# Score blocks of 32 by 32 on four column groups, attention's second product four heads at a time, and a reordered convolution

## The chip, the cores and the metric

One core of one Trainium2 chip runs the whole program. The metric is the device time of one execution in microseconds (us); for several runs it is their median. TensorE (PE) is the matrix engine, VectorE is DVE in the profile, ScalarE is ACT, GpSimd is POOL, SyncE (SP) issues most transfers.

## What is computed

Two transformer blocks follow each other on 256 tokens of width 1024, everything in float32. Two pieces matter here. In the first block each of 16 attention heads (8 "fox", 8 "swa") of width 64 computes

```python
p = jax.nn.softmax(logits, axis=-1)                  # 256 queries, causal or windowed
return jnp.einsum('bhqk,bkhd->bqhd', p.astype(v.dtype), v)
```

beside a short convolution `gate_b * conv(gate_c * u)` over 512 channels and six gates. In the second block a gated linear recurrence runs in both directions over 8 heads of 128:

```python
decay = jnp.exp(jnp.minimum(diff, 0.0)) * mask[:, :, None]
scores = jnp.einsum('bhtk,bhsk,bhtsk->bhts', qc, kc, decay)
o_intra = jnp.einsum('bhts,bhsv->bhtv', scores, vc)
```

All large weights (about 180 MB) are read once from memory. Each large product is made of three cheap products (high part by high part, high by low, low by high).

## The kernel before

**Units.** A weight of 128 by 2048 elements is a unit. SP loads it into `raw`, ACT copies it to its rounded part `whi` (`hi`, L1214), DVE forms the rest `wlo` (`lo`, L1844), PE multiplies (`unit`, L548, and `unit_tm`, L630). There are three buffers of each kind, and ACT and DVE work two units ahead of PE. Every engine has its own program, written out by hand; the engines wait for each other by counted semaphores. What stands between two units is called a slot below.

**Attention** (first block). In slot t PE does `values(t-4)`, `probs(t-3)` (three transposes, L823) and `scores(t-1)` (L811, L812). `values(i)` (L837, L838) multiplies one head's 128 tokens by 128 columns of values, of which 64 are the head's and 64 are zeros, so that two heads add up into one bank `Ob`. ACT makes exponentials and copies the turned probabilities (`pt`, two buffers, L1357); for every second head ACT and DVE split `Ob` into `y_hi` and `y_lo` (L1365, L1866). The units beside them are, in order, the convolution's `cc`, `cu`, `cb`, then six gates of two units each. DVE does the convolution as one piece after slot 5: `z` (L2035), three taps for each of four channel groups (L2039, L2043), then `lo` of the next unit.

**Recurrence scores** (second block). In each of two halves i (4 heads each), nine levels n = 0 to 8 with distances h = 0, 1, 2, 4, ..., 64, 128 are computed, one in each slot. `mix_exps` prepares on ACT and DVE the scaled keys `kt` and queries `qt` of level n and advances the running sums `xf`, `xb`, `pf`, `pb`. PE's `mix_scores` (L1026) computes for levels 0 to 7 sixteen blocks of 64 keys by 64 queries: 8 pairs, each pair's outputs on partitions 0 to 63 and 64 to 127 of a bank. DVE copies the entries that belong to the level into `an` by a mask (L2311), and at level 64 `an` into the diagonal blocks of `am` (L2306); ACT copies level 0, level 64 (L1572) and level 128 (L1578). `mix_values` (L1042) multiplies the scores `am` by `v`, 256 columns at a time.

**What sets the order.** In each recurrence slot ACT and DVE run `mix_exps(i, t)`, then `hi` or `lo` of the unit two ahead, then the copy of level t-1; PE runs the unit and then level t-1.

Of the kernel before, what the change touches and what calls it, by code (L numbers as in the profile page):

```python
# [4 lines left out]
F32 = mybir.dt.float32  # L5
F32R = mybir.dt.float32r
U8 = mybir.dt.uint8
# [25 lines left out]
def constants():  # L33
# [6 lines left out]
    for h in LEVELS[:-1]:  # L40
        same = (i[:, None] // (2 * h)) == (i[None, :64] // (2 * h))
        other = (i[:, None] // h) != (i[None, :64] // h)
        masks.append(np.tile((same & other)[:64], (2, 1)).astype(np.float32))
# [46 lines left out]
def build(nc, d, out):  # L90
# [20 lines left out]
    masks = at("masks", [P, 6, 64], U8, 91)  # L111
# [14 lines left out]
    mk = at("mk", [P, 6, 64], F32, 160)  # L126
# [4 lines left out]
    skf = at("skf", [P, 2, P], F32, 180)  # L131
    fv = [at(f"fv{u}", [P, 2, 4, P], F32, 184 + 4 * u) for u in range(2)]
# [13 lines left out]
    PT = [at(f"pt{i}", [P, 384], F32, 140.5 + 1.5 * i) for i in range(2)]  # L146
# [26 lines left out]
    Am = at("am", [P, 4, 2, T], F32, 156)  # L173
    An = at("an", [P, 8, 64], F32, 204)
# [151 lines left out]
    U["cc"], U["cu"], U["cb"] = (cols(w_in, c, 512, 8) for c in (512, 1024, 0))  # L326
    for i in range(6):
        U[f"gate{i}"] = cols(w_in, 3848 + 512 * i, 512, 8)
    wb = d["w_branch"].rearrange("a b k n -> (a b) k n")
# [80 lines left out]
    def sync(e):  # L410
# [51 lines left out]
        e.dma_start(mk[:, :, :], d["c_masks"].rearrange("p (l n) -> p l n", l=6)).then_inc(s_mk, 16)  # L462
        fetch_for("cu", "cb")
        for i in range(6):
            fetch_for(f"gate{i}")
        e.wait_ge(*pe_val.on(("attn", 15)))
        e.wait_ge(*v_split.on(("y", 15)))
# [52 lines left out]
    def tensor(e):  # L520
# [269 lines left out]
        def scores(i):  # L790
# [14 lines left out]
            if i == 8:  # L805
                e.wait_ge(*p_pad.on(("local value", 1)))
                e.wait_ge(*v_evac.on("sq"))
                e.wait_ge(*v_evac.on("sk"))
# [17 lines left out]
        def values(i):  # L826
            kind, h = heads[i]
            if kind == "fox":
                val = [fv[h % 2][:, t_, h // 2, :] for t_ in range(2)]
            else:  # L830
                val = [sv[h // 4][:, t_, :] for t_ in range(2)]
            e.wait_ge(*a_soft.on(("pt", i)))
            if i == 8:
                e.wait_ge(*a_evac.on("sv"))
            if i % 2 == 0 and i >= 2:
                e.wait_ge(*v_split.on(("y", i - 1)))
            e.matmul(Ob[:, 0:T], val[0], PT[i % 2][:, 0:T], start=i % 2 == 0, stop=False, skip_group_check=True)  # L837
            e.matmul(Ob[:, P:T], val[1], PT[i % 2][:, T:T + P], start=False, stop=True,  # L838
                     skip_group_check=True).then_inc(*pe_val.up(("attn", i)))

        def attention(t):
            if t >= 4:
                values(t - 4)
# [16 lines left out]
        linear("cb", HA, 1, None, v_evac.on("cc"), lambda i: attention(6 + i))  # L860
        for g in range(6):
            free = v_evac.on(("cu", "cb")[g]) if g < 2 else a_stat.on(("gate", g - 2))
            for i in range(2):
                unit_tm(f"gate{g}", i, HA, g % 2, free if i == 0 else None)
                attention(8 + 2 * g + i)
# [6 lines left out]
        e.wait_ge(*v_split.on(("y", 7)))  # L872
        unit_tm("br01", 0, Y, 0, a_stat.on(("gate", 4)), K=4, off=4)
        e.wait_ge(*v_split.on(("y", 15)))
# [126 lines left out]
        def mix_scores(i, n):  # L1001
# [1643 lines left out]
```

## Time and profile before

| what | value |
|---|---|
| median of 3 runs | 1052.52 us (1050.35 to 1052.54) |
| the profiled execution | 1050.1 us, of which the span from first to last instruction is 1048.3 us |
| PE matmuls | 1038.3 us busy, 99% of the span, 7132 records |
| DVE, ACT | 747.0 us (71%), 601.8 us (57%) |
| DMA | 182.84 MB, mean 174 GB/s |
| granted TensorE clock | 1.000 over the span |

A float32 product is two records of PE in the profile (a turning one is one record). Matmuls are pipelined and the ends of their records are modelled, so the distance between starts tells what a product costs, not the length of its record; a short wait of PE hides in that modelled tail, and a longer one stands in brackets only with what is left of it.

### The profile page before, as it was taken

Reading aid. Unit: us, or ns where it says so; the run is one execution under the profiler, and the core shown is the slowest. Engines: PE = TensorE matmul, PEld = TensorE weight load, DVE = VectorE, ACT = ScalarE, POOL = GpSimd, SP = SyncE. Lnnn points to the kernel's source line nnn. Section 1 sums busy time; section 2 is a strip of 40 time slices with the busy share of each in tenths; the row PEclk is TensorE's granted clock in tenths of the full one; section 3 lists DMA queues with packets and bytes.
Section 4 is the critical chain, followed back from the end, with each engine's and each line's share of the span. In section 5 each row is a group of like instructions: output and inputs, shape, how many; then the busy total and the mean of one; then the engine's idle time right before and its main releaser. Section 6 shows DMA issues by size and latency. Waiting matters only on the chain.

```text
span 1048.3 us, 16748 instructions
## 1 busy us (share of the span) xinstructions
PE 1038.3 (99%) x7132; PEld 943.7 (90%) x7132; DVE 747.0 (71%) x889; ACT 601.8 (57%) x736; POOL 8.0 (1%) x15
## 2 busy tenths in 40 slices
PE   9999999999999999999999999999999999999998
PEld 8999788889998988888899989999999888888887
DVE  5677765675654678776668898589948888776456
ACT  5564466435434565555447986698664765545443
POOL 3000000000000000000000000000000000000000
PEclk9999999999999999999999999999999999999999
DMA  9964344754543466565565555354444657554641
GB/s 295 229 187 167 121 161 161 210 193 160 201 161 122 160 217 208 188 201 172 175 215 162 161 161 162 121 161 153 139 154 152 199 170 231 176 189 159 222 160 41
DMA packets 141451, 182.84 MB, mean 174 GB/s; under 512 B 14133, under 2 KB 92065, under 8 KB 141377
## 3 DMA queue, kind: packets, MB, share of 16 engines
q1 hardware_dynamic: 141160, 181.57, 54.8%
q8 instruction: 56, 0.92, 0.3%
q10 hardware_dynamic: 216, 0.21, 0.1%
q14 instruction: 19, 0.15, 0.0%
HBM read 180.51 MB, written 1.25 MB: 173 GB/s over the span
## 4 chain that ended last, share of the span: by engine, by line
PE 88%; DVE 5%; ACT 4%; issue 2%; DMA 1%; SPq 0%; DVEq 0%; ACTq 0%
PE ps L548 26%; PE ps L581 22%; PE ps L630 15%; PE ps L583 11%; PE ps L674 2%; PE ps L1156 2%; PE ps L1026 1%; ACT whi L1214 1%; PE ps L578 1%; DVE wlo L1844 1%; PE ps L676 1%; DMA x_tm<-in_x 1%; PE ps L906 1%; PE ps L1042 1%; PE ps L928 1%
## 5 line engine op out<-in xcount | busy, mean ns | idle before, releaser
L1844 DVE TENSOR_TENSOR wlo<-raw,whi 128x2048 fp32r<-128x2048 f32 (+3 forms) x170 | 378.1, 2228 | 141.0 <-ACT whi L1214 140.5
L1214 ACT ACTIVATE whi<-raw 128x2048 fp32r<-128x2048 f32 (+1 forms) x167 | 310.5, 1863 | 84.2 <-PE ps L548 28.8
L548 PE MATMUL ps<-ha,whi 128*128 128x256 f32 x1264 | 232.1, 286 | 1.5 <-DVE wlo L1844 1.5
L581 PE MATMUL ps<-ha,whi 128*128 128x512 f32 x640 | 222.7, 395 | 0.0
L548 PEld LDWEIGHTS ps<-ha,whi 128*128 128x128 f32 x1264 | 197.6, 192 | 3.8 <-issue 1.6
L548 PE MATMUL ps<-ha,wlo 128*128 128x256 f32 x632 | 178.8, 283 | 0.0
L583 PE MATMUL ps<-ha,wlo 128*128 128x256 f32 x640 | 177.4, 277 | 0.0
L581 PEld LDWEIGHTS ps<-ha,whi 128*128 128x128 f32 x640 | 120.0, 188 | 28.0
L548 PEld LDWEIGHTS ps<-ha,wlo 128*128 128x128 f32 x632 | 121.1, 192 | 0.0
L583 PEld LDWEIGHTS ps<-ha,wlo 128*128 128x128 f32 x640 | 120.2, 188 | 0.1
L581 PE MATMUL ps<-pr,whi 128*128 128x512 f32 x330 | 115.3, 394 | 0.0
L630 PE MATMUL ps<-whi,ha 128*128 128x512 f32 x320 | 101.2, 397 | 0.2
L583 PE MATMUL ps<-pr,wlo 128*128 128x256 f32 x330 | 91.5, 277 | 0.0
L581 PEld LDWEIGHTS ps<-pr,whi 128*128 128x128 f32 x330 | 61.9, 188 | 13.7
L630 PEld LDWEIGHTS ps<-whi,ha 128*128 128x128 f32 x320 | 59.4, 188 | 13.1 <-issue 1.0
L630 PE MATMUL ps<-wlo,ha 128*128 128x512 f32 x160 | 62.5, 391 | 0.0
L583 PEld LDWEIGHTS ps<-pr,wlo 128*128 128x128 f32 x330 | 62.0, 188 | 0.0
L1513 ACT ACTIVATE silu<-silu 128x512 f32<-128x512 f32 x22 | 13.9, 633 | 62.3 <-DVE silu L2183 62.3
L1508 ACT ACTIVATE silu<-ps 128x512 f32<-128x512 f32 x22 | 13.1, 597 | 41.2 <-PE ps L583 35.3
L630 PEld LDWEIGHTS ps<-wlo,ha 128*128 128x128 f32 x160 | 30.0, 188 | 6.5
L2185 DVE TENSOR_TENSOR silu<-silu,rw 128x512 f32<-128x512 f32 x22 | 15.2, 692 | 15.9 <-ACT silu L1513 15.9
L1349 ACT ACTIVATE lb<-lb,sc 128x128 f32<-128x128 f32 x16 | 6.3, 394 | 30.6 <-DVE sc L1983 30.6
(406 smaller groups left out, 1744.2 us busy)
## 6 DMA issues: line engine op xcount, KB each, us to landing
raw<-in_w_in SPq DMA_DIRECT2D x54, 1024.0 KB, 5.2
raw<-in_w_ffn_gate SPq DMA_DIRECT2D x11, 1024.0 KB, 5.1
raw<-in_w_ffn_up SPq DMA_DIRECT2D x11, 1024.0 KB, 5.2
raw<-in_w_gate SPq DMA_DIRECT2D x11, 1024.0 KB, 5.2
raw<-in_w_up SPq DMA_DIRECT2D x11, 1024.0 KB, 5.1
raw<-in_w_xkv SPq DMA_DIRECT2D x8, 1024.0 KB, 5.0
raw<-in_w_ffn_down SPq DMA_DIRECT2D x8, 1024.0 KB, 4.9
raw<-in_w_down SPq DMA_DIRECT2D x8, 1024.0 KB, 5.1
```

What stands on the lines that cost most here:

```text
L548: mm = e.matmul(ps[0:width, m * T:(m + 1) * T], a[:, kk, m * width:(m + 1) * width], b[:, off + k, :], start=k == 0 and j == 0 and m % 2 = ...
L578: mm = e.matmul(banks[s][:, at_:at_ + T], a[:, kk, c], b[:, k, :], start=k == 0 and j == 0, stop=k == K - 1 and j == 2, skip_group_check=True)
L581: e.matmul(banks[s][:, at_:at_ + 512], wh[:, kk, c], H[2][:, :, k, :], start=k == 0, stop=False, skip_group_check=True)
L583: mm = e.matmul(banks[s][:, at_ + T:at_ + 512], wl[:, kk, c], H[0][:, k, :], start=False, stop=k == K - 1, skip_group_check=True)
L630: mm = e.matmul(banks[s][:, t * 512:t * 512 + ncol], b[:, off + k, t * P:(t + 1) * P], a[:, kk, 0:ncol], start=k == 0 and j == 0, stop=k = ...
L674: e.matmul(banks[ss[i]][:, at_:at_ + 512], wh[:, k, c], H[2][:, :, k, :], start=k == 0, stop=False, skip_group_check=True)
L1156: mm = e.matmul(where, x[:, k, t_ * P:(t_ + 1) * P], w[:, kk, a:b], start=k == 0 and j == 0, stop=k == 7 and j == 2, skip_group_check=True)
L1214: e.activation(h, r, ACT.Copy).then_inc(*hi_done.up(n))
L1508: e.activation(silu[w][:, :, :], split_sums(ss[2 * (i % 2)])[1], ACT.Copy).then_inc(*a_evac.up(f"{b}g{i}"))
L1513: e.activation(silu[w][:, :, :], silu[w][:, :, :], ACT.Silu).then_inc(*a_stat.up((f"silu {b}", i)))
L1844: e.tensor_tensor(l, r, h.bitcast(F32), ALU.subtract).then_inc(*lo_done.up(n))
L2185: e.tensor_tensor(g_, g_, rows4(Rw, 2), ALU.mult).then_inc(*v_stat.up((f"gate r {b}", i)))
```

## The change

1. **Scores.** Levels 0 to 32 (seven of the nine) become 32 blocks of 32 keys by 32 queries, four of them side by side on partitions 0, 32, 64 and 96. Levels 1 to 16 copy 8 x 32 instead of 8 x 64 elements by mask; level 32 is now four plain copies straight into `am`, and DVE copies `an` into the diagonal in four pieces in that slot, one slot earlier than before. `am` is stored with eight rows of blocks, and level 64 needs two copies instead of four.
2. **Recurrence values.** For each head the product with the second 128 tokens is two products of 128 columns instead of one of 256.
3. **Attention values.** `values` runs once for four heads, in slots 7, 11, 15 and 19, with 64 columns of values for each product; heads of a pair write partitions 0 to 63 and 64 to 127. `pt` has four buffers. The zeros that POOL wrote for values are gone. `y_hi` and `y_lo` are made four heads at a time.
4. **Convolution.** The gate 0 units come before `cb`; `cc` is scaled by the square of the row factors in one operation; the taps of one channel group each are done in slots 6 to 9, between DVE's maximum of a head and its wait for ACT's exponential; the last operations move to the slots of gates 1 and 2.
5. **One slot.** In slot (1, 1) of the recurrence ACT and DVE do `hi` and `lo` of the unit two ahead before `mix_exps`.

```diff
-            for w in range(2):
-                for m in range(4):
-                    for u in range(2):
-                        k0, q0 = w * P + 64 * u, w * P + 64 * (1 - u if h == 64 else u)
-                        mm = e.matmul(Sb[b][OWN[u], (4 * w + m) * 64:(4 * w + m) * 64 + 64], Kt[b][:, m, k0:k0 + 64],
-                                      Q_[:, m, q0:q0 + 64], start=w == 0 and m == 0, stop=True, skip_group_check=True)
+            size = 64 if h == 64 else 32
+            for m in range(4):
+                for w in range(2):
+                    for u in range(P // size):
+                        k0, q0 = w * P + size * u, w * P + size * (u ^ 1 if h >= 32 else u)
+                        mm = e.matmul(Sb[b][size * u:size * (u + 1), (2 * m + w) * size:(2 * m + w + 1) * size],
+                                      Kt[b][:, m, k0:k0 + size], Q_[:, m, q0:q0 + size], start=w == 0 and m == 0,
+                                      stop=True, skip_group_check=True)
...
-                    for w in range(2):
-                        mm = e.matmul(B_[j][:, (m % 2) * T:(m % 2 + 1) * T], v[:, w, (4 * i + m) * P:(4 * i + m + 1) * P],
-                                      Am[:, m, w, :], start=m % 2 == 0 and w == 0, stop=w == 1, skip_group_check=True)
+                    c0, vv = (m % 2) * T, [v[:, w, (4 * i + m) * P:(4 * i + m + 1) * P] for w in range(2)]
+                    e.matmul(B_[j][:, c0:c0 + T], vv[0], Am[:, 2 * m, :], start=m % 2 == 0, stop=False,
+                             skip_group_check=True)
+                    e.matmul(B_[j][:, c0 + P:c0 + T], vv[1], Am[:, 2 * m + 1, 0:P], start=False, stop=True,
+                             skip_group_check=True)
+                    mm = e.matmul(B_[j][:, c0:c0 + P], vv[1], Am[:, 2 * m + 1, P:T], start=False, stop=True,
+                                  skip_group_check=True)
...
+        def values(j):
+            e.wait_ge(*a_soft.on(("pt", 4 * j + 3)))
...
+            for t_ in range(2):
+                q_, p_ = (slice(0, T), slice(0, T)) if t_ == 0 else (slice(P, T), slice(T, T + P))
+                for n in range(4):
+                    kind, h = heads[4 * j + n]
+                    u = n % 2
+                    val = fv[u][:, t_, h // 2, OWN[u]] if kind == "fox" else sv[u][:, t_, OWN[u]]
+                    c0 = T * (n // 2)
+                    mm = e.matmul(Ob[OWN[u], c0 + q_.start:c0 + q_.stop], val, PT[n][:, p_], start=t_ == 0 and n < 2,
+                                  stop=t_ == 1, skip_group_check=True)
+            mm.then_inc(*pe_val.up(("attn", j)))
...
         def slot(u, i, t):
-            mix_exps(i, t)
-            lo(u + 2)
+            if (i, t) == (1, 1):
+                lo(u + 2)
+                mix_exps(i, t)
+            else:
+                mix_exps(i, t)
+                lo(u + 2)
             mix_scores(i, t - 1)
...
+        lo(U["gate0"][0][0] + 2)
+        attention(6, lambda: taps(0))
+        lo(U["gate0"][1][0] + 2)
+        attention(7, lambda: taps(1))
         e.wait_ge(s_mk, 16)
         e.tensor_copy(masks[:, :, :], mk[:, :, :]).then_inc(*v_stat.up("masks"))
         lo(U["cb"][0][0] + 2)
-        attention(6)
+        attention(8, lambda: taps(2))
         lo(U["cb"][1][0] + 2)
-        attention(7)
+        attention(9, lambda: taps(3))
```

On PE, attention's slot 4 before: after the last products of a unit come the values of head 0 (`pt`, `fv`), then the turning of head 1's probabilities (`lb`), then the scores of head 3.

```order
L548 MATMUL ps<-ha,wlo_57 128x256
L837 MATMUL ps<-pt_103,fv_83 128x256
L838 MATMUL ps<-pt_103,fv_83 128x128
L823 MATMUL ps<-ident,lb_101 128x128 x3
L811 MATMUL ps<-fk_81,fq_79 128x128
L812 MATMUL ps<-fk_81,fq_79 128x256
```

The same engine in slot 7 after the change, the first slot that has values:

```order
L634 MATMUL ps<-wlo_57,ha 128x512
L843 MATMUL ps<-pt_104,fv_84 64x256
L843 MATMUL ps<-pt_105,fv_85 64x256
L843 MATMUL ps<-pt_106,fv_84 64x256
L843 MATMUL ps<-pt_107,fv_85 64x256
L843 MATMUL ps<-pt_104,fv_84 64x128
L843 MATMUL ps<-pt_105,fv_85 64x128
L843 MATMUL ps<-pt_106,fv_84 64x128
L843 MATMUL ps<-pt_107,fv_85 64x128
L827 MATMUL ps<-ident,lb_102 128x128 x3
L815 MATMUL ps<-fk_80,fq_78 128x128
```

The two products of each head left its slot; eight with half as many stationary columns stand together in every fourth slot.

On DVE, the convolution before: the last scaling of a head's probabilities, `z`, four groups of three taps (the first is shown), the masks and `wlo` of the unit that PE needs next.

```order
L1994 TENSOR_SCALAR lb_101<-lb_101,sc 128x256
L2035 TENSOR_TENSOR z<-ps,cc 128x1024
L2039 TENSOR_SCALAR cc<-z,gc 128x256
L2043 SCALAR_TENSOR_TENSOR cc<-z,gc,cc 128x255
L2043 SCALAR_TENSOR_TENSOR cc<-z,gc,cc 128x254
...
L2047 CAST masks<-mk 128x384
L1844 TENSOR_TENSOR wlo_55<-raw_49,whi_52 128x2048
```

And after the change:

```order
L2055 TENSOR_TENSOR z<-ps,cc 128x1024
L1861 TENSOR_TENSOR wlo_55<-raw_49,whi_52 128x2048
...
L2000 TENSOR_SCALAR sc<-sc 128x2
L2060 TENSOR_SCALAR cc<-z,gc 128x256
L2064 SCALAR_TENSOR_TENSOR cc<-z,gc,cc 128x255
L2064 SCALAR_TENSOR_TENSOR cc<-z,gc,cc 128x254
L2010 RECIPROCAL sc<-sc 128x2
```

`wlo` now follows `z` at once, and one group of taps stands between a head's maximum (L2000) and the reciprocal that waits for ACT.

On ACT, slot (1, 1) of the recurrence before: the gate `zt`, level 1's keys and queries, `whi` of the unit two ahead, level 0's copy.

```order
L1683 ACTIVATE zt<-ps,sc 128x1024
L1544 ACTIVATE kt_141<-kf 128x512
L1545 ACTIVATE kt_141<-kb 128x512
L1553 ACTIVATE qt_139<-pf,sc 128x512
L1556 ACTIVATE qt_139<-pb,sc 128x512
L1214 ACTIVATE whi_54<-raw_51 128x2048
L1564 ACTIVATE an<-ps 128x512
```

And after the change:

```order
L1700 ACTIVATE zt<-ps,sc 128x1024
L1227 ACTIVATE whi_54<-raw_51 128x2048
L1558 ACTIVATE kt_144<-kf 128x512
L1559 ACTIVATE kt_144<-kb 128x512
L1567 ACTIVATE qt_142<-pf,sc 128x512
L1570 ACTIVATE qt_142<-pb,sc 128x512
L1578 ACTIVATE an<-ps 128x256
```

`whi` moved in front of four operations; DVE's `wlo` moved in front of its five operations of `mix_exps` in the same way.

## Rows read from the trace of the kernel before

**Rows 1.** The page: busy time, share of the span, instructions of each engine.

```profile
PE 1038.3 (99%) x7132; PEld 943.7 (90%) x7132; DVE 747.0 (71%) x889; ACT 601.8 (57%) x736; POOL 8.0 (1%) x15
```

**Rows 2.** PE by time, an attention slot: start, length, engine, line, operands, records.

```profile
85.95 0.59 PE L548 MATMUL ps<-ha,whi 128*128 128x256 f32 x2
...
91.53 0.40 PE L548 MATMUL ps<-ha,whi 128*128 128x256 f32 x2
91.77 0.28 PE L548 MATMUL ps<-ha,wlo 128*128 128x256 f32 x1
91.89 0.60 PE L837 MATMUL ps<-pt,fv 128*128 128x256 f32 x2
...
92.55 0.49 PE L823 MATMUL ps<-ident,lb 128*128 128x128 f32 x3
```

**Rows 3.** PE by time, four blocks of products between units in the second block.

```profile
604.81 0.28 PE L548 MATMUL ps<-ha,wlo 128*128 128x256 f32 x1
605.02 1.15 PE L1026 MATMUL ps<-qt,kt 128*64 128x64 f32 x32
606.10 0.73 PE L630 MATMUL ps<-whi,ha 128*128 128x512 f32 x2
...
653.01 1.95 PE L1014 MATMUL ps<-qt,kt 128*128 128x128 f32 x16
...
660.55 3.62 PE L1042 MATMUL ps<-am,v 128*128 128x256 f32 x16
...
682.87 0.28 PE L548 MATMUL ps<-ha,wlo 128*128 128x256 f32 x1
683.08 1.97 PE L1091 MATMUL ps<-wst,zv 128*64 128x128 f32 x32
684.98 0.51 PE L548 MATMUL ps<-ha,whi 128*128 128x256 f32 x2
```

**Rows 4.** PE by time, attention's middle; brackets: idle time before, and its releaser.

```profile
93.34 0.47 PE L548 MATMUL ps<-ha,whi 128*128 128x256 f32 x1
...
114.81 0.67 PE L837 MATMUL ps<-pt,fv 128*128 128x256 f32 x2 [0.52 <-DVE y_lo L1866]
...
131.96 0.58 PE L630 MATMUL ps<-whi,ha 128*128 128x512 f32 x1
...
139.08 0.58 PE L630 MATMUL ps<-whi,ha 128*128 128x512 f32 x1
```

**Rows 5.** DVE by time: a head's reciprocal, the convolution's first operation, the next `wlo`.

```profile
98.24 0.17 DVE L1991 RECIPROCAL sc<-sc 128x2 f32<-128x2 f32 x1 [1.05 <-ACT lb L1350]
...
98.90 1.22 DVE L2035 TENSOR_TENSOR z<-ps,cc 128x1024 f32<-128x1024 f32 x1
...
106.14 2.28 DVE L1844 TENSOR_TENSOR wlo<-raw,whi 128x2048 fp32r<-128x2048 f32 x1
```

**Rows 6.** DVE by time, a recurrence slot without idle time, from copy to copy.

```profile
617.25 0.73 DVE L2311 COPY_PREDICATED an<-masks,ps 128x512 f32<-128x512 uint8 x1
...
623.61 0.73 DVE L2311 COPY_PREDICATED an<-masks,ps 128x512 f32<-128x512 uint8 x1
```

**Rows 7.** PE by time, level 1's scores and the unit behind them.

```profile
715.23 1.15 PE L1026 MATMUL ps<-qt,kt 128*64 128x64 f32 x32
717.86 0.47 PE L548 MATMUL ps<-ha,whi 128*128 128x256 f32 x2 [1.48 <-DVE wlo L1844]
```

**Rows 8.** ACT by time in slot (1, 1): start of `mix_exps`, then `whi`.

```profile
709.30 0.67 ACT L1544 ACTIVATE kt<-kf 128x512 f32<-128x512 f32 x1
...
711.75 1.90 ACT L1214 ACTIVATE whi<-raw 128x2048 fp32r<-128x2048 f32 x1
```

**Rows 9.** DVE by time in slots (1, 1) and (1, 2): `mix_exps`, two `wlo`.

```profile
711.88 1.23 DVE L2284 TENSOR_TENSOR qt<-qt,q 128x1024 f32<-128x1024 f32 x1 [1.09 <-ACT qt L1556]
...
715.44 2.28 DVE L1844 TENSOR_TENSOR wlo<-raw,whi 128x2048 fp32r<-128x2048 f32 x1
...
721.18 2.28 DVE L1844 TENSOR_TENSOR wlo<-raw,whi 128x2048 fp32r<-128x2048 f32 x1
```

More of the change, by code:

```diff
@@ L39, in constants @@
     masks = []
[L40 to L43, printed above, removed]
+    for h in LEVELS[:-2]:
+        same = (i[:, None] // (2 * h)) == (i[None, :32] // (2 * h))
+        other = (i[:, None] // h) != (i[None, :32] // h)
+        masks.append(np.tile((same & other)[:32], (4, 1)).astype(np.float32))
     masks = np.concatenate(masks, axis=1)
@@ L145, in build @@
     Lb = [at(f"lb{i}", [P, 384], F32, 136 + 1.5 * i) for i in range(3)]
-    PT = [at(f"pt{i}", [P, 384], F32, 140.5 + 1.5 * i) for i in range(2)]
+    PT = [at(f"pt{i}", [P, 384], F32, kb) for i, kb in enumerate((140.5, 142, 203, 204.5))]
     small = at("small", [32, 768], F32, 120)
@@ L824, in probs @@
             mm.then_inc(*pe_turn.up(("attn", i)))
[L826 to L833, printed above, removed]
-                e.wait_ge(*a_evac.on("sv"))
[L835 to L839, printed above, removed]
+        def values(j):
+            e.wait_ge(*a_soft.on(("pt", 4 * j + 3)))
+            if j == 2:
+                e.wait_ge(*a_evac.on("sv"))
+            if j >= 1:
+                e.wait_ge(*v_split.on(("y", j - 1)))
+            for t_ in range(2):
[8 more added lines that the diff above has]
+            mm.then_inc(*pe_val.up(("attn", j)))
         def attention(t):
-            if t >= 4:
-                values(t - 4)
+            if t >= 4 and t % 4 == 3:
+                values(t // 4 - 1)
             if 3 <= t < 19:
@@ L1351, in softmax, with gate, y_hi @@
                          accum_out=mx[:, 3:4]).then_inc(*a_soft.up(("exp", i)))
+        def gate(i):
+            e.wait_ge(*whole(f"gate{i}"))
+            e.wait_ge(*v_stat.on("half r"))
+            if i == 0:
+                e.wait_ge(*v_stat.on("masks"))
+            for t_ in range(2):
+                mm = e.activation(gates[:, i, t_, :], tokens(GATE_BANK[i])[:, t_, :], ACT.Tanh, bias=zero,
+                                  scale=sc[:, 24 + t_:25 + t_])
+            mm.then_inc(*a_stat.up(("gate", i)))
         def probs(i):
             e.wait_ge(*pe_turn.on(("attn", i)))
[L1355 to L1365 removed]
+            if i >= 4:
+                e.wait_ge(*pe_val.on(("attn", i // 4 - 1)))
+            e.activation(PT[i % 4][:, :], Tb[:, 0:384], ACT.Copy).then_inc(*a_soft.up(("pt", i)))
+        def y_hi(j):
+            e.wait_ge(*pe_val.on(("attn", j)))
+            e.activation(YH[:, 4 + 2 * j:6 + 2 * j, :], wide(Ob), ACT.Copy).then_inc(*a_split.up(("y", j)))
         def attention(t):
[L1368 to L1369 removed]
+            if t >= 4 and t % 4 == 3:
+                y_hi(t // 4 - 1)
             if 3 <= t < 19:
```

171 lines of the change are left out of this document (83 added, 88 removed).

## The prediction

> **What bounds the kernel now.** I read the page first: PE is busy for 1038.3 of 1048.3 us, DVE for 71% and ACT for 57% [rows 1], and the granted clock is full throughout. So only two things move the time: PE's own work, and the few places where PE waits. For the work I read PE in order of time around each block that the change touches, from start to start, since the ends of records are modelled [rows 2, 3]. For the waits I looked where the same work takes longer than elsewhere [rows 4, 7]. Last I read DVE and ACT in the slots whose order moves, to see what becomes late [rows 5, 6, 8, 9]. Elsewhere PE, at 99%, has nothing to gain from waits, and DVE and ACT have reserve.
>
> **1. Scores, seven levels in each of two halves.** Take a block's whole cost to PE: the distance from the last record before it to the first behind it, less the usual .12 (from 91.77 to 91.89) [rows 2], plus what the first records behind it are longer than usual. A level is 606.10 - 604.81 = 1.29, less .12, plus .11 for the pair behind it (taken from the next block): 1.28 us [rows 3]. The block of L1091 has just as many records, 32, in the same two-by-two arrangement, on 128 columns: 684.98 - 682.87 = 2.11, less .12, plus .11 (.51 long, where a usual pair is .40): 2.10 us. The same number of steps with half the columns is .82 cheaper. That these pairs do run side by side is shown beside it: 32 half-width records of L1091 last 1.97, 16 full-width ones of L1014 on as many columns last 1.95.
>
> The new level has 64 records in 16 steps of four, again as many steps as today, on 32 columns instead of 64. Along the same line it costs 1.28 - .82 / 2 = .87 us, if four blocks run side by side as two do. The line's upper bound is a step that doesn't get shorter below 64 columns: gain 0. What the line leaves at no columns is 1.28 - .82 = .46; of that .20 is seen at the edges (.21 ahead of the first record instead of .12, and the .11 behind), so a step's own fixed cost is at most .26 / 16 = 16 ns. If this is a cost of each record (8 ns), twice as many records give .26 back, and a level gains .15 only. The other bound is that all .82 go; nothing speaks for it. I take the line, .41 for each of 14 levels: **5.7 us** less. Which key and query stand where costs nothing.
>
> A rule of the Trainium skill bears on this. No row here has a product on fewer than 64 columns. "TensorEngine Tiling (Array Packing)", section "Instruction Overhead", says that a product's fixed cost equals some 60 columns, and that a dimension that is small already shouldn't be tiled for throughput. By that rule 32 columns would cost as 64 do, and the first term of the sum would be about 0; it is rival B below.
>
> **2. Attention's values.** Today a head costs 92.55 - 91.89 = .66 [rows 2], sixteen times: 10.6 us. The new group of four heads has two pairs on 256 and two on 128 columns, 768 columns of pairs. L1091 has eight pairs on 128, 1024 columns for 2.10; a level has 512 for 1.28 [rows 3]; between them lie 1.69 us, four times 6.8. Gain **3.8 us**. It would be 0 only if pairs went one after the other, which L1091 contradicts.
>
> **3. Attention's waits.** From 93.34 to 131.96 PE takes 38.62 us for five units with their slots [rows 4]. Two of them are L548 units, and one such costs 93.34 - 85.95 = 7.39 [rows 2, 4]; three are L630 units at 139.08 - 131.96 = 7.12. That makes 36.14, and 2.5 us are waiting; the records bracket only a part of it, such as .52 at 114.81. The cause stands on DVE: the convolution holds it from 98.90 to 106.14, 7.2 us, before it begins the `wlo` that PE needs next [rows 5]. What follows from that DVE lateness is the split of `Ob` and the probabilities, and PE waits for both. After the change `wlo` stands right behind `z`, so it starts some 6 us earlier; the taps are four pieces of about 1.4 us, each where DVE waited for ACT's exponential, as for 1.05 at 98.24 (one operation of 1.2 us is less, too). Counting DVE's and ACT's operations up to each unit I get no less than 3 us of slack after that, an estimate, and take all **2.5 us** as gained. Bounds: 0, if another wait comes in its place, and 2.5. The split of `y` four heads at a time comes after slots 7, 11, 15 and 19 and holds the next `values`, four slots or 28 us later; the four `pt` buffers are each filled one slot after the values that free them. Both have a slot or more of time.
>
> **4. Recurrence values.** 16 records on 256 columns last 3.62, .226 each; 16 on 128 last 1.95, .122 each, the end of the last one in both [rows 3]. Per head two records on 256 become four on 128, at most 2 x .018 dearer. Eight heads: between 0 and .3, and since the ends blow up the shorter one more, **.1 us** lost.
>
> **5. DVE and ACT in the recurrence.** DVE runs without a gap there, 623.61 - 617.25 = 6.36 us per slot [rows 6]. PE's slot is a unit of 16 x .36 = 5.76 (from 91.53 to 91.89) [rows 2] and a level, 7.04 now and 6.63 after. The units of L630 are shorter: 7.12 - (7.39 - 5.76) = 5.5, thus 6.4 after. DVE's masked copy goes over half as many elements: .73 becomes .4 to .7, by half or nothing; I take .45, so a slot of 6.1. PE stays the bound, but by .3 to .5 only, where DVE had .4 to .7. Level 32 adds DVE's four copies into `am` in a slot at which DVE is 2 us early; the copies into the diagonal are only moved. Cost 0 in the middle case; were the masked copy as long as now, 6.36 against 6.4, still 0.
>
> **6. Slot (1, 1).** PE finishes level 1 at 716.3 or so and begins the unit behind it at 717.86; a level's own distance is 1.08 [rows 3], so the wait is 717.86 - 715.23 - 1.08 = 1.55 us, for the `wlo` that DVE starts at 715.44 [rows 7, 9]. ACT's four operations ahead of `whi` take 711.75 - 709.30 = 2.45 [rows 8]. After the change `whi` comes 2.45 earlier, `wlo` can start at 711.2 and ends at 713.5: that wait is gone. But the keys and queries of level 1 come 1.85 later: ACT ends them at 713.6, DVE's multiplication (started at 711.88 before) ends at 714.9, where PE wants them at 714.8, .2 late with the semaphores. The running sums that ACT needs for level 2 are later too, DVE's from 714.9 to 717.3, ACT's four operations to 718.3, DVE's next multiplication and sums to 721.7, so the `wlo` that started at 721.18 [rows 9] starts at 721.7 and ends near 724.0. PE, no longer held, is through with its next unit and level at 714.8 + .2 + .87 + 5.76 + .87 = 722.5 by the same clock, some .2 less at the edges, and waits 1.7 us. So the wait moves one unit on: 1.55 less, .2 and 1.7 more, **.4 us** lost. Bounds: a gain of 1.5 (no new wait), a loss of 1.
>
> **Sum.** 5.7 + 3.8 + 2.5 - .1 - .4 = 11.5 us off 1048.3, which is 1036.8; the profiled execution, 1.8 us longer than its span, goes from 1050.1 to 1038.6. The median of the runs, 1052.5, lies 2.4 above it, and takes the same difference: **1041.0 us**.
>
> **Rivals.**
> - **B, 32 columns cost what 64 do.** Nothing in the trace is below 64 columns; for it speaks only that the line is drawn past its end, against it that a step's fixed cost is 16 ns at most, far below what 64 columns take. The first term goes, 11.5 - 5.7 = 5.8, the late `wlo` of part 6 loses .4 less: **1046.3**, up to 1046.7.
> - **C, the other side: records are issued one after the other.** The columns' part of a level, .82, holds 32 records, 26 ns each. If that is the price of a record and not of a pair's columns, 64 records need 1.64, and a level is .82 dearer: 11.5 in 14 levels. The waits of part 6 vanish under it (1.5 back), attention and part 4 still gain 6.2: 11.5 - 1.5 - 6.2 = 3.8 slower, **1056**. From 21.5 ns a record (64 x 21.5 ns = 1.38, .56 more than now, 7.8 in all) the change stops gaining. Against it: L1091's 32 records take twice as long as a level's beyond the edges, so that today columns set the pace, and 26 ns is only a record's upper bound.
> - **D, DVE or ACT is still late in attention.** The taps stand ahead of the reciprocal, and if ACT's exponential is back before they end, `lb`, `pt` and PE follow late. The wait of 1.05 is shorter than the taps, by .4. Four slots by up to .6 us each, or the 2.5 us that I count as gone: **1043.5**.
>
> **How the numbers follow.** A .70, B .12, C .06, D .12. A alone spans 1039 to 1043, by the bounds of parts 4 to 6. For the range I take A, D and B, and 1 us below A for a level that gains more than the line: 1038 to 1047, which leaves out C and the ends. A run of this kernel can tell .2%, 2.1 us, from no change; A, B and D are all beyond it, so faster .91, with .03 for a mixture that ends near zero and .06 for C.
>
> **What would show it.** The distance around a level: .87 (A), 1.28 (B), 2.2 (C), 14 times. Its 64 records about .74 long. The values' block in attention, 1.69 in all, four times, .66 gone from the other slots. From the first unit after the convolution's `z` to the gates no wait at PE; with D one stands ahead of the turning of `lb` or of a unit. A wait of 1.7 us at the unit after level 2 of the second half instead of 1.5 after level 1. DVE's recurrence slot 6.1. The forecast fails if edges grow with four tiles instead of two, if a PE wait that I took as hidden appears once PE's slots are .41 shorter, or if the reordered DVE work delays a gate.

## The result, and the profile after

The changed kernel takes 1039.82 us in the median of 4 runs (1038.55 to 1042.71), the kernel before 1051.43 (4 runs, 1050.14 to 1052.54). The ratio on record is 0.9896, with a 95% interval of 0.9872 to 0.9920 (the two medians by themselves give 0.9890): 11.6 us less. The profiled execution has a span of 1036.7 us, where the prediction put 1036.8.

The page of the kernel after, beside [rows 1]: PE has 464 records more and is still busy for 99% of the span; DVE and ACT have hardly changed.

```profile
span 1036.7 us, 17663 instructions
PE 1027.6 (99%) x7596; PEld 934.0 (90%) x7596; DVE 745.8 (72%) x891; ACT 601.3 (58%) x728; POOL 6.6 (1%) x11
```

PE of the kernel after in order of time (start, length, line, operands, records): the first group of attention's values, two levels of scores, the block that has not changed (L1104, before L1091), and levels 1 and 2 of the second half.

```profile
97.00 0.39 PE L634 MATMUL ps<-wlo,ha 128*128 128x512 f32 x1
97.24 0.49 PE L827 MATMUL ps<-ident,lb 128*128 128x128 f32 x3
...
103.48 0.39 PE L634 MATMUL ps<-wlo,ha 128*128 128x512 f32 x1
103.80 1.52 PE L843 MATMUL ps<-pt,fv 128*64 128x256 f32 x16
105.25 0.55 PE L827 MATMUL ps<-ident,lb 128*128 128x128 f32 x3
...
591.03 0.76 PE L1034 MATMUL ps<-q,kt 128*32 128x32 f32 x64
...
597.46 0.28 PE L552 MATMUL ps<-ha,wlo 128*128 128x256 f32 x1
597.66 0.76 PE L1034 MATMUL ps<-qt,kt 128*32 128x32 f32 x64
598.36 0.50 PE L634 MATMUL ps<-whi,ha 128*128 128x512 f32 x1
...
673.50 1.97 PE L1104 MATMUL ps<-wst,zv 128*64 128x128 f32 x32
675.40 0.51 PE L552 MATMUL ps<-ha,whi 128*128 128x256 f32 x2
...
705.05 0.28 PE L552 MATMUL ps<-ha,wlo 128*128 128x256 f32 x1
705.45 0.75 PE L1034 MATMUL ps<-qt,kt 128*32 128x32 f32 x64
...
712.08 0.76 PE L1034 MATMUL ps<-qt,kt 128*32 128x32 f32 x64
714.68 0.50 PE L552 MATMUL ps<-ha,whi 128*128 128x256 f32 x2 [1.84 <-DVE wlo L1861]
```

**A level** takes .70 us from its first record to the unit behind it (597.66 to 598.36), where it took 1.08 [rows 3]: .38 less. Over half 0, from level 0's first record to that of level 128, the two traces have 591.03 to 643.37, 52.34, and before 597.99 to 653.01, 55.02: 2.68 less for seven levels, .383 each, 5.4 us for 14.

**Attention's values** stand in four blocks, each 1.77 us from the last record of a unit to the turning behind it (103.48 to 105.25), of which .24 would be there without values (97.00 to 97.24) and whose successor is .06 longer: 1.59 in all. Sixteen heads cost .66 each in the slot of [rows 2] and .65 in most others, so 10.4 against 6.4, some 3.9 to 4.0 us less; I take 3.9.

**Attention's waits** are gone: no record of PE between 85 and 203 us has a bracket. From the unit behind the first head's scores to the first record that turns `x_tm` the kernel before needs 65.43 to 210.29, 144.86 us, the one after 64.96 to 203.35, 138.39. That is 6.5 less, of which 3.9 are the values and the rest, 2.6, the waits (a remainder, not added up from single waits).

**Slot (1, 1).** Level 1 begins .40 after the last record ahead of it (705.05 to 705.45), where .21 is usual, so it waits .19; the unit behind level 2 waits 714.68 - 712.08 - .70 = 1.90. In all 2.09, where one wait of 1.55 stood [rows 7]: .5 lost.

**Recurrence values**: from level 128's first record to that of the sums behind the values, 643.37 to 660.18 us is 16.81, before 653.01 to 669.75 is 16.74: .07 lost in each half.

These make 5.36 + 6.47 - .54 - .14 = 11.15, or 11.2. The other .5 of the 11.6 lie ahead of attention, which this execution reached earlier (64.96 against 65.43). That start varies by as much among kernels that have the same work there: e4 has 65.26, e3 65.67. So the span of 1036.7 beside the forecast 1036.8 is closer than the change itself earned.

DVE of the kernel after, in order of time, beside [rows 5]: `z`, the `wlo` behind it, and the first group of taps where DVE had waited for ACT's exponential. In a recurrence slot the masked copy now takes .45 instead of .73 [rows 6], and from copy to copy it is 615.71 - 609.63 = 6.08.

```profile
96.88 1.22 DVE L2055 TENSOR_TENSOR z<-ps,cc 128x1024 f32<-128x1024 f32 x1
98.13 2.29 DVE L1861 TENSOR_TENSOR wlo<-raw,whi 128x2048 fp32r<-128x2048 f32 x1
...
101.01 0.17 DVE L2000 TENSOR_SCALAR sc<-sc 128x2 f32<-128x2 f32 x1
101.09 0.35 DVE L2060 TENSOR_SCALAR cc<-z,gc 128x256 f32<-128x256 f32 x1
101.47 1.00 DVE L2064 SCALAR_TENSOR_TENSOR cc<-z,gc,cc 128x255 f32<-128x255 f32 x2
102.51 0.17 DVE L2010 RECIPROCAL sc<-sc 128x2 f32<-128x2 f32 x1
...
609.63 0.45 DVE L2344 COPY_PREDICATED an<-masks,ps 128x256 f32<-128x256 uint8 x1
...
615.71 0.45 DVE L2344 COPY_PREDICATED an<-masks,ps 128x256 f32<-128x256 uint8 x1
```

### The profile page after: what moved, and what is told of

Its sections match the earlier page's. It is cut to its first block, busy times and chain, and to the rows that moved or that the text cites. A ratio compares the mean times of both kernels' runs of the same rounds, so it can differ in the third digit from the quotient of the medians.

```text
span 1036.7 us, 17663 instructions
## 1 busy us (share of the span) xinstructions
PE 1027.6 (99%) x7596; PEld 934.0 (90%) x7596; DVE 745.8 (72%) x891; ACT 601.3 (58%) x728; POOL 6.6 (1%) x11
## 4 chain that ended last, share of the span: by engine, by line
PE 94%; ACT 3%; DVE 2%; issue 1%; DVEq 0%; ACTq 0%
PE ps L552 29%; PE ps L585 22%; PE ps L634 16%; PE ps L587 11%; PE ps L678 2%; PE ps L1169 2%; PE ps L582 1%; PE ps L680 1%; PE ps L1034 1%; ACT whi L1227 1%; PE ps L816 1%; PE ps L913 1%; PE ps L935 1%; PE ps L644 1%; PE ps L843 1%
## 5 line engine op out<-in xcount | busy, mean ns | idle before, releaser
L585 PE MATMUL ps<-ha,whi 128*128 128x512 f32 x640 | 222.7, 393 | 0.0
L634 PE MATMUL ps<-whi,ha 128*128 128x512 f32 x320 | 101.5, 398 | 0.0
L634 PEld LDWEIGHTS ps<-whi,ha 128*128 128x128 f32 x320 | 59.5, 188 | 12.1
L634 PE MATMUL ps<-wlo,ha 128*128 128x512 f32 x160 | 62.5, 391 | 0.0
L634 PEld LDWEIGHTS ps<-wlo,ha 128*128 128x128 f32 x160 | 30.0, 188 | 6.5
L678 PE MATMUL ps<-ha,whi 128*128 128x512 f32 x64 | 22.9, 401 | 0.4 <-DVE ha L2575 0.4
```

The costliest lines, as they stand in the source:

```text
L585: e.matmul(banks[s][:, at_:at_ + 512], wh[:, kk, c], H[2][:, :, k, :], start=k == 0, stop=False, skip_group_check=True)
L634: mm = e.matmul(banks[s][:, t * 512:t * 512 + ncol], b[:, off + k, t * P:(t + 1) * P], a[:, kk, 0:ncol], start=k == 0 and j == 0, stop=k = ...
L678: e.matmul(banks[ss[i]][:, at_:at_ + 512], wh[:, k, c], H[2][:, :, k, :], start=k == 0, stop=False, skip_group_check=True)
```

## The experiments

One thing is needed to read their spans. From the turning of `x_tm` to the first record of level 0 no kernel here changes anything, and yet this work takes 387.7 us in some executions (before, after, e3, e4, e8, e10, e12) and 390.2 in the others (e1, e2, e5, e6, e7, e9, e11). The 2.5 us arise between 405 and 545 us of the trace; below they are called the longer stretch. So the traces are compared by stretches, and a span by itself only among kernels of the same kind. e3 to e11 are one execution each: what follows for them rests on distances inside a trace, not on their times.

### Are the parts what they were priced at? e1 and e2

e1 is the kernel before with the scores and the recurrence values of the change, e2 the kernel before with attention and convolution of the change; both are parts of the diff above, with no other edit.

> The kernel before with parts 1 and 2 of the change alone (32 by 32 score blocks, the recurrence values' second product in two halves), attention and slot (1, 1) as before. Theory (parts add up, and each level saves what its block is shorter): each of 14 levels costs PE .39 less, 5.4 us; the two halved products cost .1; PE reaches the unit behind level 1 of the second half .8 us earlier than before while its `wlo` is as late as before, so that wait grows from 1.55 to about 2.3. Span 4.5 us shorter than that of before, near 1043.8. Rival (DVE's slot becomes the bound once PE's is shorter): other waits of some tenths in the recurrence, span shorter by under 3.5.

Measured: 1049.09 us in the median of 8 runs (lowest 1045.66), ratio 0.9971 (0.9958 to 0.9983). By the medians that is 3.2 us less than the kernel before beside it (1052.31), by the lowest executions 4.3. The span is 1046.2, 2.5 of which are the longer stretch, so 1043.7 beside the expected 1043.8. PE in order of time, level 1 of the second half and the unit behind it:

```profile
714.84 0.76 PE L1027 MATMUL ps<-qt,kt 128*32 128x32 f32 x64
717.85 0.36 PE L548 MATMUL ps<-ha,whi 128*128 128x256 f32 x1 [2.25 <-DVE wlo L1849]
```

The wait is 717.85 - 714.84 - .70 = 2.31, .76 more than the 1.55 before, so what two shorter levels give is lost again there. No other wait of over .1 arose. By the trace the theory holds.

> The kernel before with parts 3 and 4 alone (attention's values four heads at a time, the spread convolution), the recurrence as before. Theory: the values save .63 x 16 - 1.59 x 4 = 3.7 to 4.1 us, the waits of attention (2.5) are gone; 6.2 to 6.6 us shorter, span near 1041.9; the wait behind level 1 of the second half is 1.5 as before. Rival (the two parts hinder each other or the recurrence's gain was larger than read): under 5.5 or over 7.5.

Measured: 1046.17 us (4 runs, lowest 1043.85), ratio 0.9940 (0.9919 to 0.9961); span 1044.4, without the longer stretch 1041.9, as expected. Attention's stretch is 65.28 to 203.67, 138.39 us, exactly that of the full change, and the wait behind level 1 is 713.71 - 711.08 - 1.08 = 1.55. The two halves of the change add up: 4.6 and 6.4 us less than the span before.

### What made the waits of attention? e4 and e9

e4 is the changed kernel with the twelve taps in one piece again:

```diff
+        for m in range(4):
+            taps(m)
         lo(U["gate0"][0][0] + 2)
-        attention(6, lambda: taps(0))
+        attention(6)
...
-        attention(9, lambda: taps(3))
+        attention(9)
```

> The changed kernel with the twelve taps of the convolution in one piece behind `z` again, ahead of the next `wlo`; the values stay four heads at a time. Theory (the long piece on DVE made the waits of attention): PE waits again between 103 and 135 us, 1.5 to 2.5 us in all, ahead of turned probabilities or a unit. Rival (the split of two heads' `Ob` and the two `pt` buffers made them, and these are gone with the values in fours): no wait, span as in the changed kernel within .3.

Measured: span 1038.4, 1.7 above the changed kernel, but not for this: attention's stretch is 65.26 to 203.72, 138.46 us, .07 more than in the changed kernel. .3 lie ahead of attention, and the rest, 1.4, between 675 and 775 us, where the mean granted clock was .98 in this execution instead of 1.00. DVE, then PE in order of time, and last the same place on PE in the kernel before:

```profile
98.43 0.35 DVE L2060 TENSOR_SCALAR cc<-z,gc 128x256 f32<-128x256 f32 x1
...
104.14 2.29 DVE L1861 TENSOR_TENSOR wlo<-raw,whi 128x2048 fp32r<-128x2048 f32 x1
```

```profile
106.15 0.60 PE L816 MATMUL ps<-fk,fq 128*128 128x256 f32 x2
106.58 0.36 PE L552 MATMUL ps<-ha,whi 128*128 128x256 f32 x1
```

```profile
107.89 0.60 PE L812 MATMUL ps<-fk,fq 128*128 128x256 f32 x2
108.57 0.70 PE L630 MATMUL ps<-whi,ha 128*128 128x512 f32 x2
```

The 5.7 us of taps are back in one piece, and their `wlo` ends at 106.4, just when PE is through with the scores (106.15 + .25). PE waits .2 in front of that unit, and nowhere else in attention. Before, the `wlo` ended at 108.4, .3 after PE was through, and PE waited .4 there (108.57 - 107.89 - .24) before the waits at 114.81 and 122.94 followed. My theory fell: in the changed kernel the long piece doesn't make the 2.5 us.

e9 is the other corner: the kernel before with the convolution of the change alone, values one head at a time. It is again a part of the diff; only `y_lo(t - 4)` stands in `attention(t)` for all heads.

> The kernel before with part 4 alone (gate 0's units ahead of `cb`, `cc` scaled once, the taps spread, the last operations moved); the values stay one head at a time with two `pt` buffers, and `y` is split for two heads at a time. The run with the taps in one piece but values in fours had only .2 us of waiting, so the long piece alone doesn't make the 2.5 us. Theory (two things are needed for the waits, the long piece and the tight coupling by two buffers and one `Ob`; either part of the change frees them): no wait of over .3 us here, span 2.2 to 2.5 shorter than before, 1045.9. Rival (only the looser coupling of the values in fours removes the waits): 1 us and more of waiting ahead of values between 100 and 135 us.

Measured: span 1048.0, without the longer stretch 1045.5. Attention's stretch is 65.20 to 207.54, 142.34 us, 2.5 less than in the kernel before, and no record of PE in it has a bracket. PE in order of time, at its end:

```profile
207.30 0.40 PE L634 MATMUL ps<-wlo,y_hi 128*128 128x512 f32 x1
207.54 1.91 PE L644 MATMUL ps<-ident,x_tm 128*128 128x128 f32 x16
```

So the convolution's part of the change by itself takes the waits away (e9), and the long piece put back into the changed kernel doesn't bring them back (e4). Something that e4 keeps must then be enough too. The likely one is that values no longer hang on DVE and ACT in every slot (one `Ob` that must be split after every second head, two `pt` buffers). But e4 also keeps the earlier gate 0 and the one multiplication less, and has PE busy for 1.0 us longer in the slot at issue, since four heads stand there. No run has the values in fours with the rest as before, so which of these frees PE in e4 isn't shown.

### What did slot (1, 1) cost? e3, e8 and e12

e3 puts `mix_exps` ahead of `hi` and `lo` again:

```diff
-            if (i, t) == (1, 1):
-                lo(u + 2)
-                mix_exps(i, t)
-            else:
-                mix_exps(i, t)
-                lo(u + 2)
+            mix_exps(i, t)
+            lo(u + 2)
```

> The changed kernel with part 5 undone: in slot (1, 1) `mix_exps` stands ahead of `hi` and `lo` again. Theory: the wait stands behind level 1 again and is 1.55 + 2 x .39 = 2.3 us, since two shorter levels bring PE there earlier; no wait behind level 2. Against 2.1 us in two waits with the new order the reorder is worth .2 us. Rival (the prediction's reading, in which the new order costs .4): the wait is 1.6, and the span .5 shorter.

PE of e3 in order of time, level 1 and the unit behind it:

```profile
705.88 0.76 PE L1034 MATMUL ps<-qt,kt 128*32 128x32 f32 x64
708.90 0.48 PE L552 MATMUL ps<-ha,whi 128*128 128x256 f32 x2 [2.25 <-DVE wlo L1857]
```

The wait is 708.90 - 705.88 - .70 = 2.32, and there is none behind level 2. (The span, 1039.0, has a stretch between 700 and 760 with a mean granted clock of .97.) The new order is therefore worth .2 us, 2.09 against 2.32 (e4, with the new order too, has .16 and 1.90). What costs is something else: the two shorter levels ahead bring PE there .8 earlier, to a `wlo` that is no earlier.

e8 keeps that old order, but lets DVE update `xf` and `xb` ahead of its multiplication in this slot, while it waits for ACT:

```diff
+            first = (i, n) == (1, 1)
+            if not first:
+                e.wait_ge(*a_mix.on(("qlo", i, n)))
+                if h == 1:
+                    e.wait_ge(*v_mix.on(("q", i)))
+                e.tensor_tensor(Qt[b][:, :, :], Qt[b][:, :, :], q[:, :, :], ALU.mult).then_inc(*v_mix.up(("qt", i, n)))
...
             e.tensor_tensor(Xfl, Xfl, Pfu[:, :, h - 1:h].broadcast_to(shp), ALU.add).then_inc(*v_mix.up(("xf", i, n)))
             e.tensor_tensor(Xbu, Xbu, Pbl[:, :, 0:1].broadcast_to(shp), ALU.add).then_inc(*v_mix.up(("xb", i, n)))
+                if first:
+                    e.wait_ge(*a_mix.on(("qlo", i, n)))
+                    e.wait_ge(*v_mix.on(("q", i)))
+                    e.tensor_tensor(Qt[b][:, :, :], Qt[b][:, :, :], q[:, :, :], ALU.mult).then_inc(*v_mix.up(("qt", i, n)))
```

> The changed kernel with slot (1, 1) in another order: `mix_exps` ahead of `hi` and `lo` as before the change, but DVE updates `xf` and `xb` ahead of its multiplication of `qt`, in the time in which it waits for ACT. Theory (DVE is late by its idle time there): `wlo` of the unit behind level 1 ends 1.2 us earlier than in the old order, the wait there is 1.1 us, and the next units have none; against 2.1 us now, span 1.0 shorter. Rival (ACT's chain is the bound): the wait moves on and is 2 us again.

```profile
705.64 0.76 PE L1034 MATMUL ps<-qt,kt 128*32 128x32 f32 x64
707.50 0.48 PE L552 MATMUL ps<-ha,whi 128*128 128x256 f32 x2 [1.10 <-DVE wlo L1857]
```

The wait is 1.16 (1.1 expected), and ahead of and behind level 3 stand two short ones, .12 and .05. The span is 1035.9, .8 less than the changed kernel's, though this execution reached attention .5 later. DVE's idle time was half of its lateness.

e12 also takes out of its way what nobody waits for there: the split of `bo` goes behind slot (1, 2), the gate `gb0` one slot later.

```diff
-        split_lo("bo", BO[0][:, :, :], BO[1][:, :, :], bo[:, :, :])
         gated_zg(1)
         for name, t in (("gb0", 1), ("gb1", 3)):
             for k, (u, _, _) in enumerate(U[name]):
                 slot(u, 1, t + k)
+            if name == "gb0":
+                split_lo("bo", BO[0][:, :, :], BO[1][:, :, :], bo[:, :, :])
```

> The changed kernel with `xf` and `xb` ahead of `qt` in slot (1, 1), in which `mix_exps` stands ahead of `hi` and `lo` again, and with the split of `bo` (one operation on ACT, one on DVE, 1.1 and 1.2 us) moved from ahead of slot (1, 1) to behind slot (1, 2), and the gate `gb0` on ACT one slot later. Theory (DVE is late by its idle time and by work that nobody waits for): no wait over .3 us at the units behind levels 1 and 2, 2.0 us shorter than the changed kernel, span near 1034.8, some 1.3% faster than the kernel before. Rival (the lateness moves to the next slots): 1 us of waiting behind level 2 or 3, 1.0 us shorter.

PE, then DVE of e12 in order of time:

```profile
705.91 0.76 PE L1034 MATMUL ps<-qt,kt 128*32 128x32 f32 x64
706.83 0.47 PE L552 MATMUL ps<-ha,whi 128*128 128x256 f32 x2 [0.17 <-DVE wlo L1860]
```

```profile
699.55 1.22 DVE L2399 SCALAR_TENSOR_TENSOR zg<-zt,ps 128x1024 f32<-128x1024 f32 x1
700.69 0.69 DVE L2321 TENSOR_TENSOR xf<-xf,pf 128x512 f32<-128x512 f32 x1
701.29 0.69 DVE L2322 TENSOR_TENSOR xb<-xb,pb 128x512 f32<-128x512 f32 x1
702.05 1.23 DVE L2326 TENSOR_TENSOR qt<-qt,q 128x1024 f32<-128x1024 f32 x1
...
704.40 2.29 DVE L1860 TENSOR_TENSOR wlo<-raw,whi 128x2048 fp32r<-128x2048 f32 x1
```

The wait is 706.83 - 705.91 - .70 = .22; two later ones of .05 and .11 stand ahead of units behind levels 4 and 5. Of the 2.09 us 1.7 are gone, where 2.0 were expected. The median is 1037.37 us (4 runs), against 1050.39 of the kernel before beside it: ratio 0.9876 (0.9856 to 0.9897). The span is 1035.6, 1.1 below the changed kernel's; .7 of the gain is hidden since this execution was later by that much ahead of attention (65.70 against 64.96). It is the fastest kernel of this study by its traces; the intervals of the two ratios overlap, so by the times alone that isn't shown.

### What sets the price of a block? e5, e6, e7, e10 and e11

All five are the changed kernel with other products in levels 0 to 32 (e5: in all eight levels of blocks). e6, e7, e10 and e11 don't compute the scores that the model needs; they are there for their times alone. e5 only changes the order:

```diff
-            for m in range(4):
-                for w in range(2):
-                    for u in range(P // size):
+            for u in range(P // size):
+                for m in range(4):
+                    for w in range(2):
```

> The changed kernel with the score blocks of a level in another order: all eight blocks of partitions 0 to 31, then all of 32 to 63, and so on; the same 64 records with the same operands. Theory (four records of different partitions run side by side, each at the price of its columns): next to each other stand records of the same partitions, which can't overlap, so a level takes 64 x .034 = 2.2 us and more from first record to the next unit instead of .70, and level 64 some 2.0 instead of 1.08. Rival (records are paced by issue, not by columns): .70 as now.

e6 takes 64 query columns for 32 keys:

```diff
-                        k0, q0 = w * P + size * u, w * P + size * (u ^ 1 if h >= 32 else u)
...
-                                      Kt[b][:, m, k0:k0 + size], Q_[:, m, q0:q0 + size], start=w == 0 and m == 0,
+                        k0, q0 = w * P + size * u, w * P + 64 * (u * size // 64)
...
+                                      Kt[b][:, m, k0:k0 + size], Q_[:, m, q0:q0 + 64], start=w == 0 and m == 0,
```

> The changed kernel with 64 query columns for each of the 32 key columns of levels 0 to 32 (the product has twice the columns; what is copied of it is not the needed block, so the output is not the reference's). Theory (a step costs by its columns, however many blocks stand side by side): a level takes 1.08 us from its first record to the next unit, as a pair step on 64 columns did before. Rival (64 records are paced by their number): .70 to .80.

e7 takes 64 keys and 32 queries, two blocks side by side:

```diff
-                    for u in range(P // size):
...
-                                      Kt[b][:, m, k0:k0 + size], Q_[:, m, q0:q0 + size], start=w == 0 and m == 0,
+                    for u in range(2):
+                        k0, q0 = w * P + 64 * u, w * P + 64 * u
+                        mm = e.matmul(Sb[b][64 * u:64 * (u + 1), (2 * m + w) * size:(2 * m + w + 1) * size],
+                                      Kt[b][:, m, k0:k0 + 64], Q_[:, m, q0:q0 + size], start=w == 0 and m == 0,
```

> The changed kernel with levels 0 to 32 as pairs of 64 keys by 32 queries: 32 records in 16 steps on 32 columns (half of each product's needed entries are left out, so the output is not the reference's). Theory (the columns set a step's price down to 32): .70 us from first record to the next unit, as with four side by side. Rival 1 (half as many records cost less): .45 to .60. Rival 2 (a record has a floor near 64 columns, and only the four-wide arrangement hides it): 1.0.

e10 takes all 128 keys and 64 queries, one product at a time (eight products, 16 records):

```diff
+                        mm = e.matmul(Sb[b][:, (2 * m + w) * 64:(2 * m + w + 1) * 64], Kt[b][:, m, w * P:(w + 1) * P],
+                                      Q_[:, m, w * P:w * P + 64], start=w == 0 and m == 0, stop=True,
```

> The changed kernel with levels 0 to 32 as 8 products of 128 keys by 64 queries on all partitions: 16 records (only a part of what they make is the needed block, so the output is not the reference's). Pairs with 64 stationary and 32 moving columns cost as much as with 64 and 64 (.0585 a step), so a step may be priced by the larger of stationary and moving columns. Theory (larger of the two): 16 records at .111, 1.7 to 1.8 us from first record to the next unit. Rival (moving columns set it down to 64, and only below is there a floor): 16 at .058, .94 to 1.08.

e11 takes 32 keys and 16 queries, four side by side:

```diff
-                                      Kt[b][:, m, k0:k0 + size], Q_[:, m, q0:q0 + size], start=w == 0 and m == 0,
...
+                                      Kt[b][:, m, k0:k0 + size], Q_[:, m, q0:q0 + (size if size == 64 else 16)], start=w == 0 and m == 0,
```

> The changed kernel with only 16 query columns for each of the 32 by 32 blocks (half of the needed scores are left out, so the output is not the reference's). Theory (a step costs by the larger of stationary and moving columns, here 32): .70 us from first record to the next unit, as with 32 columns. Rival (by the moving columns): .45 to .55.

Their single executions took 1056.79, 1044.91, 1044.92, 1049.70 and 1042.65 us (e5, e6, e7, e10, e11). Level 1 of the first half in each of them, in this order, PE in order of time: the level, and the first record of the unit behind it. Then come level 64 of e5 and, from the kernel before, the unit behind the block of L1014, which starts at 653.01 [rows 3]. In the operands 128*32 is the stationary side (rows by columns), 128x32 the moving one.

```profile
601.91 1.91 PE L1034 MATMUL ps<-qt,kt 128*32 128x32 f32 x64
603.75 0.50 PE L634 MATMUL ps<-whi,ha 128*128 128x512 f32 x1
```

```profile
600.71 1.10 PE L1035 MATMUL ps<-qt,kt 128*32 128x64 f32 x64
601.74 0.50 PE L634 MATMUL ps<-whi,ha 128*128 128x512 f32 x1
```

```profile
600.82 1.13 PE L1034 MATMUL ps<-qt,kt 128*64 128x32 f32 x32
601.88 0.50 PE L634 MATMUL ps<-whi,ha 128*128 128x512 f32 x1
```

```profile
599.20 1.90 PE L1033 MATMUL ps<-qt,kt 128*128 128x64 f32 x16
600.90 0.47 PE L634 MATMUL ps<-whi,ha 128*128 128x512 f32 x1
```

```profile
600.62 0.74 PE L1034 MATMUL ps<-qt,kt 128*32 128x16 f32 x64
601.29 0.50 PE L634 MATMUL ps<-whi,ha 128*128 128x512 f32 x1
```

```profile
647.51 1.90 PE L1034 MATMUL ps<-qt,kt 128*64 128x64 f32 x32
649.34 0.50 PE L552 MATMUL ps<-ha,whi 128*128 128x256 f32 x2
```

```profile
654.71 0.48 PE L548 MATMUL ps<-ha,whi 128*128 128x256 f32 x2
```

Put together, with the rows of before and after (us from the block's first record to the next unit):

| kernel | stationary, moving columns | side by side | records, steps | us |
|---|---|---|---|---|
| after, L1034 | 32, 32 | 4 | 64, 16 | .70 |
| e11 | 32, 16 | 4 | 64, 16 | .67 |
| e6 | 32, 64 | 4 | 64, 16 | 1.03 |
| before, L1026 | 64, 64 | 2 | 32, 16 | 1.08 |
| e7 | 64, 32 | 2 | 32, 16 | 1.06 |
| before and after, L1091 | 64, 128 | 2 | 32, 16 | 1.90 |
| e10 | 128, 64 | 1 | 16, 16 | 1.70 |
| before, L1014 | 128, 128 | 1 | 16, 16 | 1.70 |
| e5 | 32, 32 | 1 | 64, 64 | 1.84 |
| e5, level 64 | 64, 64 | 1 | 32, 32 | 1.83 |

A step costs by the larger of its two sides: about 106 ns at 128 columns (1.70 / 16), 57 at 64 (1.83 / 32), 29 at 32 (1.84 / 64). Halving the moving columns alone gives next to nothing (e7 against before, e10 against L1014, e11 against after), doubling them alone costs what a side of 64 costs (e6). Blocks side by side take .1 to .25 us more than 16 such steps, with no trend in their size (.24, .17 and .20 for L1034, L1026 and L1091, .12 and .15 in e6 and e7; an estimate from the table). And the blocks run side by side only while neighbours in PE's queue lie on different partitions: the same 64 records in e5's order take 1.84 instead of .70. The rivals of e5, e6, e10 and e11 fell; of e5's theory the order came true, but not the size, 1.84 where it said 2.2 and more. In e7 my theory fell, that the moving columns set the price down to 32. Rival 2's size came true (1.06 where it said 1.0), but not its reason: e5 issues 64 records on 32 moving columns one after the other at 29 ns each, where a floor near 64 columns would need 57, and in e10 64 moving columns cost 106. One thing stays open. Below 32 moving columns e11 can't tell the price of 32 stationary ones from a floor of the step near 29 ns; e7 and e10, with 64 and 128 stationary columns, are what shows the stationary side.

The Trainium skill has this, on "TensorE: Matmul & The Clock Gate": under "LDWEIGHTS (loading the stationary operand)" it gives the load a time that grows with the stationary columns, whatever the rows, and under "Back-to-back issue gap" it says that both the load and the product set the distance. Worked out from its figure, an estimate: 107 ns for 128 columns, 53 for 64, 27 for 32. The steps above agree, 106, 57 and 29. The Trainium skill's rule on "TensorEngine Tiling (Array Packing)", "Instruction Overhead", by which a product on 32 columns would last as long as one on 60, isn't what was seen: with 32 stationary columns a level on 32 moving ones takes .70 us, on 64 (e6) 1.03.

## Why the prediction was right, point by point

- **Scores** (5.7 forecast, 5.4 measured). The size came out, but only half of the mechanism was right, and that it sufficed was luck. The line from L1091 to a level varied the moving columns alone, from 128 to 64, with 64 stationary ones; e7 shows that the same line goes no further. That 32 columns cost .70 is due to the stationary side, which the change halved as well. Had it halved the query columns alone, the gain would have been .02 a level (e7), .3 us in all instead of 5.7. The Trainium skill's sentence that I weighed there pointed to rival B. The level's .70 us beside 1.03 in e6 decides against it as I applied it; with 64 stationary columns 32 moving ones do cost what 64 do, for another reason.
- **Attention's values** (3.8 and 3.9). The interpolation at 768 columns held, 1.59 for 1.69, since all blocks in it have 64 stationary columns and at least as many moving ones.
- **Attention's waits** (2.5 and 2.6). The size held, the cause only in part. "The cause stands on DVE: the convolution holds it" is right in that spreading it was enough (e9, short pieces and no wait). But e4 has the long piece and waits .2 only, so the piece needs the rest of the old order beside it, and the gain would have come without the spread taps.
- **Recurrence values** (.1 forecast, .14 measured lost).
- **DVE's slot** (6.1 and 6.08) stayed below PE's, 6.38 between the levels of L634 units.
- **Slot (1, 1)** (.4 and .5). The places of both waits were right, .2 and 1.7 forecast, .19 and 1.90 measured. But that the new order costs .4 is a wrong reading of this sum: without it the wait would be 2.32 (e3). The cost comes from PE's shorter levels.
- **Rivals.** B (nothing gained by 32 columns) and C (a price for each record, 26 ns) are refuted: 64 records take .70 us, 11 ns each with the edges. D's wait ahead of `lb` or a unit didn't come; the pieces of taps let ACT's exponential be back first, and the reciprocal starts at 102.51 right behind them, but no wait at PE came of it.
- **The sum** was 11.5, measured 11.2 and .5 ahead of attention that the change didn't make. The forecast median of 1041.0 came from a median of before, 1052.5, that lay 2.4 above the profiled execution; of the executions since, several lie near 1050.1. The two groups lie about as far apart as the longer stretch is long, 2.5 us. That it makes them isn't shown, as only one execution of each kernel has a trace.

## What to carry to other kernels

In this kernel a product's price was set by the larger of its stationary and its moving columns. Fewer moving columns than stationary ones gave nothing (1.06 against 1.08). The score blocks gained because both sides shrank and four of them shared a step, attention's values because two products of 64 stationary columns shared one where half of 128 had been zeros. Either way the blocks must write different partitions and be issued in turn over these (e5, in another order, takes 1.84 us instead of .70). And when PE's work ahead of a wait gets shorter, the wait grows by the same: look at each wait that is left, and first let the late engine do what it can do while it is idle, then take from its way what nobody waits for (e8, e12).

## What the runs showed of the hardware that I had not expected

- 64 stationary columns with 32 moving ones cost as much as with 64 (1.06 and 1.08 us for 16 steps), 128 with 64 as much as with 128 (1.70 both).
- What the stationary side costs is shared by four neighbouring blocks too: 16 steps of four in .70 us, where the same records one after another need 1.84.
- The same work from the turning of `x_tm` to level 0 takes either 387.7 or 390.2 us, with the granted clock shown as 1.00 between 400 and 550 us in both. Seven of the fourteen traces have the one and seven the other; the difference grows evenly between 405 and 545 us. What decides it stayed open.
